# Differential attention: rotary queries and keys made in feature layout, rotated on VectorE

## What is computed

```python
qkv = h @ w_qkv                                   # h: normed x, 512 x 1024
q, k, v = jnp.split(qkv, 3, axis=-1)
q = q.reshape(b, s, DA_HEADS, 2, DA_HEAD_DIM)     # 8 heads, 2 halves, 64
k = k.reshape(b, s, DA_HEADS, 2, DA_HEAD_DIM)
q = jnp.concatenate([apply_rope(q[..., :DA_ROT], cos, sin), q[..., DA_ROT:]], axis=-1)   # DA_ROT = 16
k = jnp.concatenate([apply_rope(k[..., :DA_ROT], cos, sin), k[..., DA_ROT:]], axis=-1)
...
sc = jnp.einsum('bqhcd,bkhcd->bhcqk', qb, k) * scale     # scale = 1/8
p = masked_softmax(sc, chunk_mask)
a = p[:, :, 0] - lam * p[:, :, 1]
```

## Time and profile before

| | us |
|---|---|
| median of 3 runs | 1744.02 (1743.98 to 1744.8) |
| profiled execution | 1744.46 |
| its span | 1742.7 |
| TensorE busy in it | 1727.3 (99%) |
| VectorE, ScalarE, GpSimd busy | 1089.5, 784.5, 134.4 |

### The profile page before, as it was taken

How to read it: one execution, slowest core, us unless ns; L and a number is a source line. 1 busy time by engine, 2 the same in 40 slices (tenths; PEclk the granted TensorE clock), 3 DMA queues, 4 the chain that set the end, 5 groups by cost and what they waited for, 6 DMA issues and landing times.

```text
span 1742.7 us, 22591 instructions
## 1 busy us (share of the span) xinstructions
PE 1727.3 (99%) x8782; PEld 1458.2 (84%) x8782; DVE 1089.5 (63%) x1719; ACT 784.5 (45%) x1398; POOL 134.4 (8%) x138
## 2 busy tenths in 40 slices
PE   9999999999999999999999999999999999999998
PEld 7888888888888888888888888889888888888887
DVE  5788644344346766685864764665888676376375
ACT  5553532232235555544532432446876554244244
POOL 2003200000005100002000000022110200000000
PEclk9999999999999999999999999999999999999999
DMA  5212333333333222222233333323111233333331
GB/s 169 73 50 83 96 97 97 97 97 97 97 97 97 74 70 64 61 73 85 89 99 97 97 97 98 97 82 102 36 42 49 81 92 97 98 98 96 98 123 66
DMA packets 128355, 152.78 MB, mean 88 GB/s; under 512 B 9286, under 2 KB 101992, under 8 KB 128248
## 3 DMA queue, kind: packets, MB, share of 16 engines
q1 hardware_dynamic: 128088, 151.26, 28.3%
q10 hardware_dynamic: 160, 0.07, 0.0%
HBM read 148.61 MB, written 2.10 MB: 86 GB/s over the span
## 4 chain that ended last, share of the span: by engine, by line
PE 94%; DVE 3%; ACT 1%; issue 1%; DMA 1%; POOL 0%; ACTq 0%; DVEq 0%; POOLq 0%
PE bk L1913 24%; PE bk L1915 23%; PE bk L1914 23%; PE bk L1942 5%; PE bk L1944 4%; PE bk L1943 4%; PE bk L1918 4%; PE bk L2040 2%; PE bk L2001 1%; PE bk L2074 1%; PE bk L2073 1%; DVE WL L2105 0%; PE bk L2028 0%; PE bk L2030 0%; PE bk L2029 0%
## 5 line engine op out<-in xcount | busy, mean ns | idle before, releaser
L1913 PE MATMUL bk<-R,WH 128*128 128x512 f32 x1844 | 723.9, 393 | 1.9 <-DVE R L2111 1.6
L1915 PE MATMUL bk<-R,WL 128*128 128x512 f32 x1844 | 718.2, 389 | 0.0
L1914 PE MATMUL bk<-R,WH 128*128 128x512 f32 x1844 | 717.9, 389 | 0.0
L2105 DVE TENSOR_TENSOR WL<-RAW,WH 128x1024 fp32r<-128x1024 f32 (+4 forms) x278 | 343.4, 1235 | 482.7 <-ACT WH L2307 481.8
L2307 ACT ACTIVATE WH<-RAW 128x1024 fp32r<-128x1024 f32 (+4 forms) x278 | 288.0, 1036 | 605.3 <-PE bk L1915 547.0
L1913 PEld LDWEIGHTS bk<-R,WH 128*128 128x128 f32 x1844 | 346.4, 188 | 73.4 <-issue 2.7
L1915 PEld LDWEIGHTS bk<-R,WL 128*128 128x128 f32 x1844 | 346.1, 188 | 72.7
L1914 PEld LDWEIGHTS bk<-R,WH 128*128 128x128 f32 x1844 | 346.4, 188 | 69.6
L1942 PE MATMUL bk<-WH,R 128*128 128x256 f32 (+4 forms) x432 | 146.1, 338 | 0.3 <-DVE KT L2111 0.3
L1944 PE MATMUL bk<-WL,R 128*128 128x256 f32 (+4 forms) x432 | 140.6, 326 | 0.0
L1943 PE MATMUL bk<-WH,R 128*128 128x256 f32 (+4 forms) x432 | 140.5, 325 | 0.0
(11 more groups left out here) (170 smaller groups left out, 1502.0 us busy)
## 6 DMA issues: line engine op xcount, KB each, us to landing
RAW<-in_ffn_w_up_dram SPq DMA_DIRECT2D x176, 256.0 KB, 3.1
RAW<-in_ffn_w_down_dram SPq DMA_DIRECT2D x44, 512.0 KB, 3.7
RAW<-in_w_gate_dram SPq DMA_DIRECT2D x44, 256.0 KB, 2.8
RAW<-in_w_up_dram SPq DMA_DIRECT2D x44, 256.0 KB, 3.1
RAW<-in_w_down_dram SPq DMA_DIRECT2D x22, 512.0 KB, 3.7
RAW<-in_da_w_qkv_dram SPq DMA_DIRECT2D x32, 256.0 KB, 2.9
RAW<-in_w_out_dram SPq DMA_DIRECT2D x8, 512.0 KB, 3.7
RAW<-in_da_w_qkv_dram SPq DMA_DIRECT2D x8, 512.0 KB, 3.5
```

The source lines that it names most:

```text
L1913: e.matmul(dst, lh, rh, start=start, stop=False)
L1914: e.matmul(dst, lh, rl, start=False, stop=False)
L1915: return e.matmul(dst, ll, rh, start=False, stop=stop)
L2105: e.tensor_tensor(low, sides(st.n, RAW[:, r, 0:m]), high.bitcast(F32), ALU.subtract).then_inc(on["wlo_dve"], 1)
```

## The change

Queries and keys are made by `gemm_f`, with features on the partitions, in four banks (two of queries, two of keys) of 128 features by 512 tokens. `rot_copy` copies each bank on ScalarE into one of five 512-column pieces of `TOKS[0]`. Then VectorE makes, for each: `rot_swap` (a stream shuffle that exchanges rows 0 to 7 with rows 8 to 15 of a quadrant, into one of three pieces of `TOKS[1]`), `rot_cosine` and `rot_sine` (products with two tables in `TOKS[1]`), and `rot_add`. All of it has rank 1.5. The splits then read SBUF in place of a bank; the factor 1/8 of the queries goes into their split. The tables are loaded once (512 KB, `rot_load`) and multiplied once by the norm of the tokens, spread over the partitions by one more `over` (`rot_spread`). The steps `tok_qk`, `heads` and `rope` of this stage go, and a small VectorE product (`eighth`). The mask of the latent keys (`mask_key`) now waits for the latent tokens.

```diff
-            def ev_qk(t, bk, done):
-                free = tok_free if g < 2 else before.ups
-                while N.rooted is None or len(free) < 4:
-                    yield None
-                st = yield step("tok_qk", tok=g % 2, t=t, bank=bk.i, rq=N.r8[:, t:t + 1], rk=N.r[:, t:t + 1],
-                                after=counts([done, free, N.rooted]))
-                G.toks.append(st.act)
+            def ev_rotated(m, bk, done):
+                y = yield from taken_from(rot.whole)
+                st = yield step("rot_copy", dst=rot.at(y), bank=bk.i, after=counts([done, y.free]))
                 put_bank(bk, st.act)
...
+                spawn(rotated(m, y, st.act), 1.5)
+
+            def rotated(m, o, copied):
+                while rot.spread is None or m < 2 and G.Q[m].h is None:
+                    yield None
+                z = yield from taken_from(rot.swapped)
+                st = yield step("rot_swap", dst=rot.at(z), src=rot.at(o), after=counts([copied, z.free]))
+                swapped = st.dve
+                st = yield step("rot_cosine", o=rot.at(o), after=[swapped, rot.spread])
+                turned = st.dve
+                st = yield step("rot_sine", z=rot.at(z), after=[swapped, rot.spread])
+                st = yield step("rot_add", z=rot.at(z), o=rot.at(o), after=[st.dve, turned])
+                rot.swapped.put(z, st.dve)
+                if m < 2:
+                    lo = yield from split_pair(G.Q[m], rot.at(o), [st.dve], 0.125)
+                else:
+                    while before and not before.valued:
+                        yield None
+                    i = G.kbase + 4 * (m - 2)
+                    lo = yield from halves(KT[:, i, :], KT[:, i + 1, :], rot.at(o), [st.dve], None, [kfree[i + x] for x in range(4)])
...
-                spawn(turn_in())
-                yield from gemm_t(N.X, 8, 512, ev_qk)
+            yield from gemm_f(N.X, 8, 4, ev_turned if kind == "fg" else ev_rotated)
...
+            b = yield from bank()
+            st = yield step("over", bank=b.i, r=N().r, after=counts([b.free, N().rooted]))
+            st = yield step("rot_spread", bank=b.i, after=counts([st.pe, (s_rot, 16)]))
...
+                    e.tensor_tensor(rot.cos, BK[st.bank][:, :], rot.cos, ALU.mult).then_inc(on["rot_spread_dve"], 1)
+                    e.tensor_tensor(rot.sin, BK[st.bank][:, :], rot.sin, ALU.mult).then_inc(on["rot_spread_dve"], 1)
...
+                    e.stream_shuffle(st.dst, st.src, [x ^ 8 if x < 16 else x for x in range(32)]).then_inc(on["rot_swap_dve"], 1)
...
+                    e.tensor_tensor(st.o, st.o, rot.cos, ALU.mult).then_inc(on["rot_cosine_dve"], 1)
...
+                    e.tensor_tensor(st.z, st.z, rot.sin, ALU.mult).then_inc(on["rot_sine_dve"], 1)
...
+                    e.tensor_tensor(st.o, st.o, st.z, ALU.add).then_inc(on["rot_add_dve"], 1)
```

More of the change, by code:

```diff
@@ L691, in total @@
                     r.r = r.r1 = o
[L692 to L695, removed]
                     r.rooted = rooted
@@ L1211, in in_line, with taken_from, rotation @@
                 spawn(fill_by(t, pairs), 0)
+        rot = Group()
+        rot.spread, rot.cos, rot.sin = None, flat(1)[:, 0:S], flat(1)[:, S:2 * S]
+        rot.whole, rot.swapped = Ring(5), Ring(3)
+        for x in rot.swapped.fr:
+            x.i += 5
+        rot.at = lambda x: flat(0)[:, x.i * S:x.i * S + S] if x.i < 5 else flat(1)[:, (x.i - 3) * S:(x.i - 2) * S]
+        def taken_from(ring):
+            while not ring.fr:
+                yield None
+            return ring.get()
+        def rotation(N):
+            for x in rot.whole.fr:
+                x.free = list(tok_free)
+            emit("rot_load", after=[])
+            landing(s_rot, free_at["pe"] + 20000.0)
+            while N() is None or N().rooted is None:
+                yield None
+            b = yield from bank()
+            st = yield step("over", bank=b.i, r=N().r, after=counts([b.free, N().rooted]))
+            st = yield step("rot_spread", bank=b.i, after=counts([st.pe, (s_rot, 16)]))
+            put_bank(b, st.dve)
+            rot.spread = st.dve
         def qkv_group(G, g, N, kind, spent, prior=None, before=None):
@@ L1506, in ev @@
             def ev(t, bk, done):
-                while NM.rooted is None or len(Gs[2].ups) < 4:
+                while NM.rooted is None or any(len(G.ups) < 4 for G in Gs):
                     yield None
                 st = yield step("tok_lat", t=t, c0=c0, width=width, bank=bk.i, r=NM.r[:, t:t + 1],
-                                after=counts([done, Gs[2].ups, NM.rooted]))
+                                after=counts([done, [G.ups for G in Gs], NM.rooted]))
                 lat.toks.append(st.act)
@@ L1554, in kpe @@
             toks = lat.toks[0:4]
-            masked = yield step("mask_key", after=[])
+            masked = yield step("mask_key", after=toks)
             cs, sn = (CN[:, o:o + 64].rearrange("p (t c) -> p t c", c=16) for o in (C_CML, C_SML))
@@ L1589, in ev_q @@
             def ev_q(t, bk, done):
-                used = Gs[3].ups if g == 0 else lat.ups if g == 1 else before.qups
+                used = [x for G in Gs for x in G.ups] if g == 0 else lat.ups if g == 1 else before.qups
                 while lat.rooted is None or len(used) < (6 if g == 1 else 4):
@@ L1719, in da_norm @@
                 return last.n
+            last.n = None
+            spawn(rotation(lambda: last.n))
             yield from ffn(N2, value_plain, da_norm)
@@ L2462, in gpsimd_program @@
                 elif k == "mask_key":
+                    for done in st.after:
+                        w.wait_ge(*done)
                     src = CN[:, C_MK:C_MK + 16].rearrange("p (t c) -> p t c", c=4)
```

107 lines of the change are left out of this document (52 added, 55 removed).

## The result

The changed kernel takes 1752.47 us (median; 1751.81 to 1753.69) beside 1744.09 us for the kernel before on the same chip: the ratio is 1.0047, 95% interval [1.0035, 1.0059]. It is 8.4 us slower, where 3.5 us faster was forecast, and it lies 4 us above the range. The profiled execution has a span of 1750.8 us in place of 1742.7.

What follows compares the result with a forecast made beforehand. TensorE, busy for 99% of the span, was taken as the bound. Of 7.4 us possible, 3.9 become a wait for the last head, so 3.5 are gained: 1740.5 us against 1744.02; range 1736.0 to 1748.5, the forecast's own 1738.5 to 1742.0.

Steps and rivals of the forecast that it cites:

- VectorE decides, and the kernel is slower: Rival: from 23.5 us of delay to group 3's scores, each further microsecond is lost; 1748.5 us at 28 us; chance 0.17.
- the signs named: Right: no transposes, scores 19 to 22 us after gemm, one last wait; wrong: idle TensorE before earlier groups' scores.
- What TensorE saves: Differential attention stage: four groups' transposes go, 7.00 us, one `over` is added, 0.44; net 6.56 us, at most 7.4.
- What a step costs on VectorE: Rotation per bank: three operations of 687 ns and a shuffle of 683 ns; 11.0 us per group.
- the estimate of 600: Shuffle time in ns estimated from the skill's page, as a quarter of about 2400 ns; the forecast itself took 683.
- So no backlog grows from group to group. The first three groups cost nothing: VectorE at 90% before 740 us is not over the limit; TensorE's other gemms cover scores some 4 us later.
- The way of 20 us for group 3: From the end of group 3's query-key gemm to its first scores: 20 us, before 16.0; bounds 17 and 28.
- 9.5 us are other work: VectorE's work besides low parts in the 19.3 us to 738.60, all assumed ahead of group 3's rotation.
- From the scores to the last projection: Group 3's first scores to the waiting last projection: 54.5 us kept, less 0.6, so from 735.7 to 789.6.
- all of it is kept: Rival: the way stays within 16 us, or the last two heads run faster without competing projections; 7.4 us, 1736.6; chance 0.17.

Runs made afterwards that it cites:

- the lighter kernel: Changed kernel with the VectorE low parts of the stage's weights cut from 1024 columns to 128; 1737.93 us, 0.9962 against the kernel before.
- e8: Changed kernel with 49 products of zeros on TensorE where it waits for the last heads; 1751.12 us, 1.0039 against the kernel before.

## Why the prediction was wrong

Wrong: the sign. Of the rivals, "VectorE decides, and the kernel is slower" is what happened, with 0.17; its price, 1748.5 us at a way of 28 us, was too small. Of the signs named, the transposes went and idle time in front of a score bundle of an earlier group came (0.96 us before 729.76), as did five waits in place of one.

- **What TensorE saves: right.** 6.56 us, at most 7.4 with the idle time, were worked out; where VectorE has room the change gives 7.2 us.
- **What a step costs on VectorE: right.** A group is 4 x (0.735 + 3 x 0.683) = 11.1 us; 11.0 was forecast. The shuffle takes 735 ns, within the bounds of 544 and 963; the estimate of 600 from the Trainium skill's page "VectorE: DVE Perf Modes" ("The perf-mode tier table") was too low.
- **"So no backlog grows from group to group. The first three groups cost nothing": failed, the smaller part.** First scores came at 598.85, 647.05 and 695.99 in place of 588.37, 638.47 and 688.53. Two groups alone should give 2 x 1.75 - 0.44 = 3.1 us (with the whole `over`; the expectations took shares of the net 6.56) and gave 2.1; three should give 4.8 and gave 0.4. At a load of 85%, with the new work ranked behind the rest, the work was delayed; the 15% left were not spare room for it. In group 0 the eight products of `settle`, not counted by me, also stand ahead of the rotation (573.70 to 580.17).
- **The way of 20 us for group 3: failed, and it decided.** The forecast had the gemm end at 715.7 and the scores at 735.7. The gemm ended at 711.73, 4 us earlier still, since the second head of group 2 begins only behind it; the scores came at 751.35. The term that was too small is "9.5 us are other work", read from a window of the kernel before. In the changed kernel VectorE does 37.4 us of work in that time, of which some 11.5 are rotation and low parts of queries and keys: 26 us are other work. The window of before showed what VectorE had done in 19.3 us, not what was queued. A longer way lets in more: projections of finished groups go on meanwhile, and each sends a sum (ten of L2124 in the 39.6 us, 6.6 us) and each load of weights a split (five, 6.1 us), many of them ahead of the rotation. In the run with the last group alone, where nothing is handed on, it was 12.8 us. In the lighter kernel 715.9, 736.5 and 20.7 us were measured, with some 9 us of other work: the sum holds where its term of 9.5 does.
- **From the scores to the last projection: 53.9 us forecast, 47.4 measured** (798.76 - 751.35). The last heads did run faster, with fewer projections beside them (15 sums on VectorE in that stretch, 24 before); this half of the rival "all of it is kept" held, and so scores 12.8 us later than before cost 5.7 us at the last projection. That the missing sums are the reason was not tested.
- **The clock was not foreseen.** It fell with the waits and stayed full when they were filled (e8); the first 4.8 us of the last projection hold 2.3 us of loss.

Whether another mix of VectorE's queue could keep more than 2.1 us with the full computation stays open; three other rankings of the rotation did not.

## What to carry to other kernels

Before moving work to an engine at 80%, don't ask whether its sum fits: take the stretch between producer and consumer and add all that is ranked ahead and will arrive while the new work waits. The last of several pipelined groups has no gemm of its kind behind it to cover a delay, so try such a change on all groups but the last ones first; here two of four gained 2.1 us and the last one alone lost 7.1. To find whether an engine's load or a chain's length is the cause, take unrelated work away from that engine in both kernels.

## What the runs showed of the hardware

A stream shuffle of 128x512 float32 takes 735 ns (724 to 746), and the mask load ahead of it 13 ns. TensorE's granted clock fell to its lower level around stretches of broken work (busy for 1.64 of 4 us from 780 to 784, mean granted clock 0.89 there and 0.68 from 784 to 788); after the last projection had gone on at 798.76 its steps were 0.43 us until 803.59 and 0.23 us after 803.86. With 49 products that nobody reads in the waits, it was full (1.00) in each window of 4 us from 780 to 808. In the run with GpSimd's products, VectorE's products of two SBUF operands took up to 1432 ns where one overlapped, and 675 to 687 otherwise.
